# Reordering around w_out, the tenth round's down units, two late weight splits, and the gate of GpSimd's first turn

## The reference, cut to what matters

```python
mod = silu(c) @ w_ada + b_ada                      # shift, scale, gate, six vectors
x = x + gt1 * (concat(y_rwkv, y_pool) @ w_out)     # w_out
h = rmsnorm(x, norm2_g) * (1.0 + sc2) + sh2
u = h @ w_up
y = conv_b + sum_j conv_w[j] * shifted(u, j)
val, gate = split(y)
x = x + gt2 * ((silu(gate) * val) @ w_down)        # up and down units
x = rmsnorm(x, norm_f_g)                           # then the second block: its norm, kv units, ...
```

## Time and profile before

| | value |
|---|---|
| median of three runs | 2870.54 us |
| the profiled execution | 2878.32 us |
| its span, first to last instruction | 2876.5 us |
| mean granted clock of TensorE | 0.952 of full speed |
| TensorE busy | 2656.5 us, 92% |
| VectorE busy | 1848.3 us, 64% |
| ScalarE busy | 1082.2 us, 38% |
| GpSimd busy | 1088.5 us, 38% |
| moved by DMA | 568.72 MB, 198 GB/s |

### The profile page before, as it was taken

One profiled execution on the slowest core, in us unless ns is written; L12 is line 12 of the kernel. 1 busy time (PEld: TensorE's weight loads), 2 busy tenths in 40 slices (PEclk: granted clock), 3 DMA queues, 4 the chain that ended last, 5 costly groups with the idle time before them and its releaser, 6 DMA issues.

```text
span 2876.5 us, 51512 instructions
## 1 busy us (share of the span) xinstructions
PE 2656.5 (92%) x22896; PEld 2496.4 (87%) x22896; DVE 1848.3 (64%) x2055; ACT 1082.2 (38%) x1237; POOL 1088.5 (38%) x611
## 2 busy tenths in 40 slices
PE   5589968959899999999996999999999999999997
PEld 2179946739899999999995999999998998999997
DVE  0137574446788888888887766566445774776454
ACT  1234322223433434444434544344333434434342
POOL 0292000000498998999994076774000000000001
PEclk7589989969999999999998999999999999999999
DMA  8867645726677887777773685776666665666664
GB/s 317 294 179 204 176 176 178 236 89 188 178 231 239 243 243 244 242 240 236 242 240 88 169 212 173 223 204 181 181 189 181 170 164 176 169 168 162 182 185 117
DMA packets 759198, 568.72 MB, mean 198 GB/s; under 512 B 46496, under 2 KB 645664, under 8 KB 758848
## 3 DMA queue, kind: packets, MB, share of 16 engines
q1 hardware_dynamic: 758976, 565.42, 67.0%
HBM read 563.29 MB, written 2.10 MB: 197 GB/s over the span
## 4 chain that ended last, share of the span: by engine, by line
PE 77%; DVE 9%; DMA 5%; POOL 4%; ACT 3%; issue 1%; SPq 0%; DVEq 0%; POOLq 0%; ACTq 0%
PE bank L721 16%; PE bank L725 16%; PE bank L722 16%; PE bank L705 5%; PE bank L706 5%; PE bank L707 5%; DVE w_low L1595 2%; PE bank L919 2%; DMA ada<-w_ada 2%; PE bank L694 2%; ACT w_high L1211 2%; PE bank L760 2%; PE bank L759 2%; PE bank L758 2%; POOL prod_e L594 1%; POOL acc_e L595 1%
## 5 line engine op out<-in xcount | busy, mean ns | idle before, releaser
L1595 DVE TENSOR_TENSOR w_low<-ring,w_high 128x2048 fp32r<-128x2048 f32 x388 | 954.7, 2463 | 427.8 <-ACT w_high L1211 420.4
L721 PE MATMUL bank<-act_high,w_high 128*128 128x256 f32 x4480 | 1098.3, 285 | 54.5 <-DVE act_low L1894 33.3
L722 PE MATMUL bank<-act_low,w_high 128*128 128x256 f32 x4480 | 1092.6, 284 | 0.0
L721 PEld LDWEIGHTS bank<-act_high,w_high 128*128 128x128 f32 x4480 | 863.0, 193 | 57.3 <-DVE act_low L1894 33.3
L1211 ACT ACTIVATE w_high<-ring 128x2048 fp32r<-128x2048 f32 x388 | 737.7, 1903 | 413.8 <-DMA ring<-w_up 166.7
L722 PEld LDWEIGHTS bank<-act_low,w_high 128*128 128x128 f32 x4480 | 863.3, 193 | 0.1
L725 PE MATMUL bank<-act_high,w_low 128*128 128x256 f32 x4480 | 583.2, 283 | 0.4 <-DVE w_low L1595 0.4
L725 PEld LDWEIGHTS bank<-act_high,w_low 128*128 128x128 f32 x4480 | 557.4, 192 | 0.7 <-DVE w_low L1595 0.6
L594 POOL TENSOR_SCALAR prod<-adf,cact 128x512 f32<-128x512 f32 x165 | 348.6, 2113 | 52.7 <-DMA adf<-w_ada 37.5
L595 POOL TENSOR_TENSOR acc<-prod,acc 128x512 f32<-128x512 f32 x165 | 307.9, 1866 | 13.8
L608 POOL TENSOR_TENSOR sumf<-sqf 128x256 f32<-128x256 f32 x1 | 0.7, 747 | 795.7 <-ACT sqf L1576 795.7
(11 more groups left out here) (427 smaller groups left out, 3309.7 us busy)
## 6 DMA issues: line engine op xcount, KB each, us to landing
ring<-w_in SPq DMA_DIRECT2D x182, 1024.0 KB, 5.8
ring<-w_up SPq DMA_DIRECT2D x88, 1024.0 KB, 6.0
ada<-w_ada SPq DMA_DIRECT2D x76, 1024.0 KB, 7.1
adf<-w_ada SPq DMA_DIRECT2D x44, 1024.0 KB, 8.2
ring<-w_down SPq DMA_DIRECT2D x44, 1024.0 KB, 5.4
ring<-w_out SPq DMA_DIRECT2D x16, 1024.0 KB, 5.9
adg<-w_ada SPq DMA_DIRECT2D x64, 256.0 KB, 5.7
ring<-w_mla SPq DMA_DIRECT2D x16, 1024.0 KB, 5.3
```

What stands on the lines that cost most here:

```text
L721: pe.matmul(o, wh[:, j], AH[:, j, :], start=j == 0, stop=False, skip_group_check=True)
L722: pe.matmul(o, wh[:, j], AL[:, j, :], start=False, stop=False, skip_group_check=True)
L1595: v.tensor_tensor(WL[s][:, 0:WIDE[n]], ring[s][:, 0:WIDE[n]], f32(WH[s][:, 0:WIDE[n]]), ALU.subtract)\
```

## The change

In words, in the order of the diff. (1) Rounds 1 to 9 keep their down units in the middle. Round 10 has only its up units; the down units of round 9 follow behind all of them and ahead of those of round 10, in the order of units, in SyncE's, TensorE's, ScalarE's and VectorE's lists. (2) ScalarE's loop over w_out is written differently. (3) In the last four groups ScalarE makes the high halves of kv units 0 and 1 between the squares of groups 2 and 3; before, one ahead of group 2 and one ahead of group 3. VectorE makes the low half of kv 0 ahead of the results of group 3 (before: of group 2) and that of kv 1 behind all results (before: ahead of group 3). (4) In VectorE's loop over w_out the low half of unit k + 2 is made behind the result of unit k, and not ahead of it. (5) The gate for SyncE's quarters 0 and 1 of round 0 is set behind `h_tiles` and the low half of up unit 3. (6) `down_sums` and `evicted` are helpers; `down_sums(9)` runs behind the rounds.

```diff
--- before.py
+++ after.py
@@ -71,8 +71,9 @@
     keys += [("w_out", k) for k in range(16)]
     for i in range(12):
         up = [("up", i, k) for k in range(8)] if i < 11 else []
-        down = [("down", i - 1, s) for s in range(4)] if i else []
+        down = [("down", i - 1, s) for s in range(4)] if 0 < i < 10 else []
         keys += up[:4] + down + up[4:]
+    keys += [("down", i, s) for i in (9, 10) for s in range(4)]
     keys += [("kv", k) for k in range(5)]
     keys += ATTENTION + [("gl", k) for k in range(1, 16)]
     keys += DILATED + [("w_o", k) for k in range(16)]
@@ -493,12 +494,13 @@
                 if i:
                     ups(i, (2, 3))
                 ada_quarter(w, first, 1)
-                if i:
+                if 0 < i < 10:
                     downs(i - 1)
                 ups(i, (4, 5))
                 ada_quarter(w, first, 2)
                 ups(i, (6, 7))
                 ada_quarter(w, first, 3)
+            downs(9)
             downs(10)
             for k in range(4):
                 load(("kv", k), w_in2[:, 3072 + P * k:3200 + P * k])
@@ -1046,10 +1048,10 @@
                 elif i < 11:
                     for k in range(4):
                         std(("up", i, k), k)
-                if i:
+                for r in (() if i in (0, 10) else (9, 10) if i == 11 else (i - 1,)):
                     for s in range(4):
-                        down(i - 1, s)
-                    ada(acc2[(i - 1) % 2])
+                        down(r, s)
+                    ada(acc2[r % 2])
                 if i < 11:
                     for k in range(4, 8):
                         std(("up", i, k), k % 4)
@@ -1374,10 +1376,11 @@
             act.activation(AH[:, 0:8, :], tmp2[:, :, :], ACT.Copy)
             act.activation(AH[:, 8:16, :], yp[:, :, :], ACT.Copy).then_inc(act_to_dve, 1)
             sqrt_table()
+            ahead(UNIT["w_out", 2])
             for k in range(16):
-                ahead(UNIT["w_out", k] + 2)
                 act.wait_ge(bank_free[k % 4], freed[UNIT["w_out", k]])
                 act.activation(sq[:, k, :], xT[:, k, :], ACT.Square).then_inc(sq_done, 1)
+                ahead(min(UNIT["w_out", k] + 3, UNIT["up", 0, 1]))
             root(4, rstd, 1.0 / D)
             ahead(UNIT["up", 0, 2])
             h_high(3 * DT, hf2)
@@ -1404,12 +1407,14 @@
                             .then_inc(bank_free[k % 4], 1)
                     if k % 2 == 0 and (k or i):
                         finish()
-                    if k == 3 and 0 < i < 11:
+                    if k == 3 and 0 < i < 10:
                         for s in range(4):
                             ahead(UNIT["down", i - 1, s] + 2)
                     if k == 1 and i == 11:
                         break
 
+            for s in range(4):
+                ahead(UNIT["down", 9, s] + 2)
             act.wait_ge(f_free, 4 * (N_FIRST + N_FFN))
             from_dve()
             act.activation(sinM[:, :], ang[:, 0, :], ACT.Sin)
@@ -1422,8 +1427,8 @@
             act.wait_ge(act_seq, B.up("act_seq"))
             ahead(UNIT["down", 10, 3])
             for s in range(4):
-                if s > 1:
-                    ahead(UNIT["kv", s - 2])
+                if s == 3:
+                    ahead(UNIT["kv", 1])
                 if s:
                     act.wait_ge(sums_ready, s + 1)
                 for m in range(2):
@@ -1917,8 +1922,8 @@
 
             seq(v.tensor_copy(posf[:, :], post[:, :]))
 
+            ahead("w_out", 0, to=1)
             for k in range(16):
-                ahead("w_out", k)
                 if k in (2, 8):
                     seq(v.tensor_scalar(ang[:, k // 8, :], posf[:, :], pr("freq", k // 8 * 2), None, ALU.mult))
                     angle(k // 8, tang[:, k // 8, :], 0.25, 1.5707964)
@@ -1928,6 +1933,7 @@
                 v.scalar_tensor_tensor(xT[:, k, :], bank[k % 4][:, 0:T], mod[:, 2 * DT + k:2 * DT + k + 1],
                                        xT[:, k, :], ALU.mult, ALU.add).then_inc(bank_free[k % 4], 1)
                 B.up(f"bank_free{k % 4}")
+                ahead("w_out", k)
 
             def taken(b):
 
@@ -1937,9 +1943,9 @@
                 taken(s)
             moved(4)
             seq(v.reciprocal(rstd[:, :], rstd[:, :]))
-            v.memset(small[:, 62:63], 0.0).then_inc(gate_sp, 1)
             h_tiles(3 * DT, hf2, ("up", 0, 2))
             ahead("up", 0, 3, to=0)
+            v.memset(small[:, 62:63], 0.0).then_inc(gate_sp, 1)
 
             def conv(i, n):
                 raw_tile(n % 4)
@@ -1966,6 +1972,28 @@
 
                     ins.then_inc(dve_to_pe, 1)
                     v.wait_ge(dve_to_pe, B.up("dve_to_pe"))
+
+            def evicted(s, m, ins):
+
+                if m == 0:
+                    ins.then_inc(bank_free[s], 1)
+                    B.up(f"bank_free{s}")
+                else:
+                    ins.then_inc(x_free[4 + s % 2], 1)
+                    B.up(f"x_free{4 + s % 2}")
+
+            def down_sums(r):
+                for s in range(4):
+                    ahead("down", r, s)
+                    unit("down", r, s)
+                    for m, o in ((0, bank[s]), (1, bank[4 + s % 2])):
+                        d = dacc[:, 4 * s + 2 * m:4 * s + 2 * m + 2, :]
+                        u = o[:, :].rearrange("p (a b) -> p a b", a=2)
+                        if r:
+                            evicted(s, m, v.tensor_tensor(d, u, d, ALU.add))
+                        else:
+                            evicted(s, m, v.tensor_copy(d, u))
+                ada_take(5 * DT + 4 * r)
 
             for i in range(12):
                 for n in range(8):
@@ -1981,42 +2009,34 @@
                         gated((n // 2 - 1) % 4)
                     if n == 1 and i == 11:
                         v.memset(small[:, 61:62], 0.0).then_inc(dve_to_act, 1)
-                    if n == (3 if i < 11 else 1) and i:
-                        for s in range(4):
-                            if i < 11:
-                                ahead("down", i - 1, s)
-                            else:
-                                if s < 2:
-                                    ahead("down", 10, 2 + s, to=0)
-                                else:
-                                    ahead("kv", s - 2, to=0)
-                                for k in range(4 * s, 4 * s + 4):
-                                    seq(v.scalar_tensor_tensor(xT[:, k, :], dacc[:, k, :], mod[:, 5 * DT + k:5 * DT + k + 1],
-                                                               xT[:, k, :], ALU.mult, ALU.add))
-                            unit("down", i - 1, s)
-                            for m, o in ((0, bank[s]), (1, bank[4 + s % 2])):
-                                d = dacc[:, 4 * s + 2 * m:4 * s + 2 * m + 2, :]
-                                u = o[:, :].rearrange("p (a b) -> p a b", a=2)
-                                if i == 1:
-                                    ins = v.tensor_copy(d, u)
-                                elif i < 11:
-                                    ins = v.tensor_tensor(d, u, d, ALU.add)
-                                else:
-                                    for k in range(4 * s + 2 * m, 4 * s + 2 * m + 2):
-                                        ins = v.scalar_tensor_tensor(xT[:, k, :], u[:, k % 2, :],
-                                                                     mod[:, 5 * DT + k:5 * DT + k + 1], xT[:, k, :],
-                                                                     ALU.mult, ALU.add)
-                                if m == 0:
-                                    ins.then_inc(bank_free[s], 1)
-                                    B.up(f"bank_free{s}")
-                                else:
-                                    ins.then_inc(x_free[4 + s % 2], 1)
-                                    B.up(f"x_free{4 + s % 2}")
-                        ada_take(5 * DT + 4 * (i - 1))
-                        if i == 10:
-                            v.wait_ge(ada_free, N_EARLY + 1 + 10 + 1)
-                        if i == 11:
-                            break
+                    if n == 3 and 0 < i < 10:
+                        down_sums(i - 1)
+                    if n == 1 and i == 11:
+                        break
+            down_sums(9)
+            for s in range(4):
+                taken(s)
+            for b in (4, 5):
+                v.wait_ge(x_free[b], B.at(f"x_free{b}") + 1)
+            v.wait_ge(ada_free, N_EARLY + 1 + 10 + 1)
+            for s in range(4):
+                if s < 2:
+                    ahead("down", 10, 2 + s, to=0)
+                elif s == 3:
+                    ahead("kv", 0, to=0)
+                tiles = range(4 * s, 4 * s + 4)
+                for k in tiles:
+                    seq(v.scalar_tensor_tensor(xT[:, k, :], dacc[:, k, :], mod[:, 5 * DT + k:5 * DT + k + 1], xT[:, k, :],
+                                               ALU.mult, ALU.add))
```

(9 more changed lines are left out.)

## The result

The forecast was 2877 us and no change. The changed kernel took **2879.77 us**, a median of 20 runs (2873.45 to 2888.93), against 2873.44 us of the kernel before in 20 runs on the same chip (2862.59 to 2882.41). The ratio is **1.0025, interval 1.0013 to 1.0036**: slower by 6.3 us between the medians and by 7.2 us by the ratio, well inside 1%, and inside the forecast range. The forecast was 2870.54 + 6.2; over 20 runs the kernel before has a median 2.9 us higher than over those three.

What follows compares the result with a forecast made beforehand. TensorE, busy for all of a steady 70.00 us round, was taken as the bound. The gate's +9.7 us and the end's -3.5 gave +6.2, a forecast median of 2877 us, range 2862 to 2892.

Steps and rivals of the forecast that it cites:

- The tie at the first down unit: Round 1: TensorE's first down unit starts 12.1 us after GpSimd ends turn 0, whatever TensorE did before.
- w_out: End of w_out: unit 15's result starts 3.7 us earlier, and up 1's low half just fits ahead of the reciprocal.
- rival D: End of w_out: up 1's low half holds the reciprocal, the norm starts up to 2.3 us later, +9; no chance given.
- The tiles without GpSimd: First norm's tiles: without GpSimd beside them VectorE's stretch takes 18.5 us, not 22.4; 1.1 us gained for TensorE.
- The gate: Turn 0: GpSimd starts 14.6 us later, its turn takes 60 us, the first down unit comes 9.7 us later.
- rival A: Turn 0 is short, near 50 us, so the gate costs nothing and the end's -3.5 us is left; chance 0.17.
- Rival C: Turn 0 stays at 65 us, the first quarter lands late, the end gains nothing: +19 us, 2890; chance 0.15.
- Rival B: GpSimd paces every round, with turns over 70 us: +33 us or more, 2904; chance 0.04.
- Round 10: Round 10's new order: the first square comes 1.2 to 3.2 us earlier, 2.5 taken.
- Down 9: Round 9's down units: a new wait of about 5 us ahead, then 25.1 us, so down 10 starts as now.
- The last splits: Last weights between squares: moving kv 0's halves gains between nothing and 2.3 us, 1 us taken.
- The end's balance: Round 10 and the last weights between squares together: -3.5 us, ends 0 and -6.

Runs made afterwards that it cites:

- e7: The changed kernel with the loads of each round's first two down units ahead of quarter 1 in SyncE's list: 2873.53 us, ratio 1.0005 against before.
- b2: The kernel before run once more, unchanged, for a second trace: turn 0 took 61.7 us; no median, one run.
- e1: The changed kernel with the gate of quarters 0 and 1 back ahead of the norm's tiles: 2869.07 us, ratio 0.9993 against before.
- e2: The kernel before with only the gate moved behind the norm's tiles and the low half of up unit 3: 2886.43 us, ratio 1.0056.
- e9: The changed kernel with half of GpSimd's turn 0 left out, so part of mod isn't computed: 2868.14 us, ratio 0.9965 against before.
- e4: The kernel before with only round 10's order changed, its down units behind all up units: 2876.21 us, ratio 1.0007.
- e5: The kernel before with only the last weight splits of kv 0 and 1 moved: 2874.69 us, ratio 0.9997.
- e8: The kernel before with w_out's results first, the last splits moved and two down loads ahead of quarter 1 in every round: 2869.09 us, ratio 0.9977.
- e6: The kernel before with w_out's results ahead of the low halves and the last splits moved: 2868.55 us, ratio 0.9983.
- e3: The kernel before with only w_out's results put ahead of the low halves in VectorE's loop: 2871.65 us, ratio 0.9993.

## Why the prediction was right, point by point

*The tie at the first down unit: right.* 12.2 us from turn 0's end to the first down unit, as read from the earlier trace rows. e7 cut the tie on SyncE and the first down unit came 3.9 us earlier, only 8.3 us behind the turn's end.

*w_out: right.* The result starts at the unit's end; the low half fits ahead of the reciprocal, so rival D falls. Before the tiles begin it takes 744.30 - 739.88 = 4.4 us behind the unit's last matmul; 4.7 was booked.

*The tiles without GpSimd: VectorE's stretch right, TensorE's share too small.* The gate opened 18.4 us behind the first tile (18.5 booked): VectorE saved 4.0 of its 22.4 us. The Trainium skill, "SBUF — State Buffer" ("Who interferes with whom"), has the two engines shut each other out; the trace agrees: a tile instruction of VectorE (L1669, now L1674) took up to 1.56 us beside GpSimd before and 0.48 us here. The first up result came 762.49 - 744.30 = 18.2 us behind the first tile; 19.6 was booked from the second norm, 20.7 measured before: 2.5 us less, where 1.1 was booked. The second norm was a poor price: it now takes 1592.15 - 1573.96 = 18.2 us itself, and 18.2 in b2 too, whose code is that of before. The two busy rows below are of the same 17 us in it, before and after:

```profile
1573.00:1590.00 17.00, 14.23 (x100) 13.93 (x101) 15.80 (x32) 9.55 (x17) 0.00 (x0) 0.90 0.00 1
```

```profile
1575.00:1592.00 17.00, 14.21 (x112) 13.89 (x113) 15.80 (x32) 9.58 (x17) 0.00 (x0) 1.00 0.00 1
```

The granted clock was 0.90 there before and 1.00 after, and in the same busy time TensorE did 100 matmuls before and 112 after (columns as in the earlier trace rows). So the row used as a price had a piece of slow clock in it. The mean clock alone doesn't tell this, though: over the first norm of the changed kernel (745 to 762 us) it is 0.90 as well, and that norm takes 18.2 us. There the clock is 0.50 from 745.6 to 748.8, ahead of a wait of TensorE for VectorE's tiles (1.07 us at 753.0, where the second norm has 2.0) that takes the loss up; in the second norm of before it is 0.50 from 1582.3 to 1585.6, behind the last such wait.

*The gate: right in its size and its way.* GpSimd started 28.2 us behind the last matmul of w_out's last unit (28.4 booked), its turn took 59.0 (60), with seven low halves beside it in place of nine (eight booked). The first down unit came 8.6 us later than before against +9.7. A piece of luck is in it: the working starts from a turn of 65.0 us, and the same code also gives 61.7 (b2), from which the same working would have led to 56.7. e1 and e2 show that this is the whole loss, and e9 that it comes from the turn's length: at 32 us the loss is gone, as rival A asks for a turn under 50. Rival C's price, 65 us beside a late gate, showed in no trace: all four complete turns behind a late gate took 58.9 to 60.3 us. Rival B falls with rounds 2 to 9, which have no wait; e2 alone shows a piece of it, 3.0 us in one round. The waits between 780 and 847 were foreseen as four or five of 2 to 6 us; there were four of 1.2 to 6.2.

*Round 10: here a step failed.* Down 9 was right: a wait of 4.5 us (5 booked), its start 660.2 us behind the first down unit (660.8 booked). The step "Down 9 takes 4 x 5.8 + 1.9 = 25.1, so down 10 starts at 1523, as now" was wrong. Down 9 took 1529.26 - 1499.46 = 29.8 us, of which 3.5 are the wait at 1516.19. So down 10 started 690.8 us behind the first down unit (1530.07 - 839.31), where 685.9 was booked. Down 9's third unit needs a bank of the first, and VectorE frees that only here:

```profile
1510.49 0.42 DVE L1968 TENSOR_TENSOR hid_low<-hfu,hid_high 128x256 fp32r<-128x256 f32 x1 [0.48 <-ACT hid_high L1395]
...
1512.29 2.55 DVE L1600 TENSOR_TENSOR w_low<-ring,w_high 128x2048 fp32r<-128x2048 f32 x1 [1.25 <-ACT w_high L1213]
1514.77 1.27 DVE L1993 TENSOR_TENSOR dacc<-bank,dacc 128x512 f32<-128x512 f32 x2
```

I had named `hid_low` as work that would be "long done". It was, but the same VectorE instructions now stand ahead of down 9's results, where before TensorE waited for them: the wait changed its name and fell from 6.8 to 3.5 us. The hidden tile isn't all of it. From the end of `hid_low` (1510.91) to the result (1514.77) VectorE waits 1.25 us for the third unit's high half, which stands behind `hid_high` in ScalarE's list, and makes its low half: `down_sums` puts the low half ahead of the result, the order that part (4) of the change turned around in w_out. TensorE needs that low half too, before the third unit can start. No run tried the other order here. Together with the new 4.5 ahead of down 9, the first square came 1.4 us later than before, counted from the first down unit, instead of 2.5 earlier. e4 shows the same as a zero.

*The last splits: mechanism right, too small.* From the first square to the end of the second sum it is 1555.00 - 1537.09 = 17.9 us after and 20.0 before: 2.1 us, where 1 was booked; e5 has 2.7 for the whole of the part (2.3 against b2). GpSimd after, second sum (before it was 5.09 and 3.38 for the same eight instructions):

```profile
1548.51 3.19 POOL L632 TENSOR_TENSOR sumy<-sumy,sqy 128x256 f32<-128x256 f32 x4 [3.05 <-ACT sqy L1442]
1551.79 3.15 POOL L632 TENSOR_TENSOR sumx<-sumx,sqx 128x256 f32<-128x256 f32 x4
1555.00 0.10 POOL L633 MEMSET small<- 128x1 f32 x1
```

VectorE's low half of kv 0 no longer runs beside this sum, and GpSimd gets through it faster. I had priced the half as work in VectorE's and ScalarE's order, not as something that slows GpSimd.

*The end's balance.* First square +1.4, second sum -2.1, third sum -0.2, TensorE's sum matmuls +0.8 (they ran at clock 0.50, the 1.2 GHz level; before at 0.68 on the mean), the tiles -1.4: in sum -1.5, where -3.5 was booked. With +8.6 that makes the 7.1 us. The +0.8 and the -1.4 aren't the change's: b2, with the code of before, has the same two against the first trace of before. Without them the end gained about 1 us.

*How near the sum came.* The forecast of +6.2 us stands against 6.3 to 7.2 measured, but its two terms missed in opposite ways: the gate cost 1.1 us less than booked and the end gained 2.0 us less. That the sum is off by only 1 us is in part luck.

*What stays open.* What moves a low half of VectorE by the 0.2 us that go with the length of turn 0 (last section); the 1.9 us of e7 behind the start of down 9; what the other order in `down_sums` would give; and whether e8 is faster than e6, whose intervals overlap widely.

## What to carry to other kernels

Where an engine's long job ends just as a load of another job leaves, look in the issuing queue's list for the order that ties them: here a quarter for GpSimd stood ahead of the first down unit, and each microsecond by which GpSimd's turn ended later than before went through. A job moved off a critical stretch must have slack at its other end, and that is read from the trace before the move. And when a wait for an operand is removed by doing something else first, ask what that something else needs from the same engine: the instructions that were waited for are still in the list, and the next buffer comes free only behind them.

## What the runs showed of the hardware

**GpSimd's turn of 31 arithmetic instructions beside VectorE has two lengths.** It took 64.9 to 65.0 us in four traces with an early gate (before, e1, e5, e6) and 61.6 to 61.7 in four (before again, e3, e4, e8). The lengths go with no edit: before is in both groups. They do go with one order. Up to 23 us behind its start the turn is alike in all eight. Then GpSimd's sixth sum (L595) and VectorE's third low half start almost together, in before and in before again:

```profile
783.36 2.29 DVE L1595 TENSOR_TENSOR w_low<-ring,w_high 128x2048 fp32r<-128x2048 f32 x1 [0.53 <-ACT w_high L1211]
...
783.39 3.41 POOL L595 TENSOR_TENSOR acc<-prod,acc 128x512 f32<-128x512 f32 x1
```

```profile
775.97 1.29 POOL L595 TENSOR_TENSOR acc<-prod,acc 128x512 f32<-128x512 f32 x1
...
776.06 3.35 DVE L1595 TENSOR_TENSOR w_low<-ring,w_high 128x2048 fp32r<-128x2048 f32 x1 [0.65 <-ACT w_high L1211]
```

In the four long turns the low half starts 0.03 to 0.13 us ahead of the sum, and the sum takes 3.3 to 3.4 us; in the four short ones it starts 0.08 to 0.22 us behind, the sum takes 1.29 us and the low half 3.2 to 3.4. That is eight traces out of eight, but no run forced the order, so it is a strong sign and no proof. Behind the first instruction of the turn, five took over 3.4 us in before and three in before again, where most of the products take 1.62. In the second, the first down unit came 13.5 us behind the turn instead of 12.1, since the w_down load took 8.69 us in place of 7.40, so only 2.2 of the 3.3 us arrive.

**A VectorE instruction slows GpSimd and is slowed by it.** A product of 128x512 took 1.57 us on GpSimd where VectorE stood idle and up to 3.74 in turn 0 beside low halves; a low half took 2.28 us alone and up to 3.35 beside the turn.

**How long a load takes varies with what left before it.** The first w_down load landed after 7.40 us behind one quarter. Up unit 4, issued at 763.76 behind two quarters, landed at about 775.72, when ScalarE starts on it: 12.0 us. What left just before isn't all of it: in before again the same w_down load took 8.69 us behind one quarter.
